# Two-layer hybrid decoder step on one core: where the second layer's modulation is loaded and computed, at what rate the convolution taps run, and which engine scales the prompt softmax

## The reference

```
mod   = silu(c) @ w_ada + b_ada ;  shift, scale, gate = split(mod, 3)     # c: 1 + 8 rows, w_ada 2048 x 6144
h     = rms_norm(x, norm_g) * (1 + scale) + shift
zq, zk, zv, zqi, zki, zwi, zga, zglu, zgc, zmerge = split(h @ w_in)
q, k  = rope(rms_norm(..)) ; qi, ki = rope(..)                            # indexer: 16 heads of 64
score = sum_heads(relu(qi . ki) * wi) ; keep the top k keys per query     # 128 (prompt), 256 (sample)
attn  = softmax(q . k over the kept keys) @ v
u     = za * sigmoid(zb) ; d = causal depthwise conv of u, 31 taps ; d = silu(layer_norm(d))
out   = (sigmoid(zma) * ((attn * silu(zga)) @ w_attn_out) + sigmoid(zmb) * ((d * silu(zgc)) @ w_conv_out)) @ w_out
x     = x + gate * out
```

## Time and profile before

| | |
|---|---|
| three runs, median (lowest, highest) | 3971.25 us (3962.26, 3978.71) |
| profiled execution, its own time | 3962.51 us |
| its span, first to last instruction | 3960.7 us |
| mean granted TensorE clock | 0.954 |
| TensorE busy | 3610.7 us (91%) |
| VectorE busy | 1882.9 us (48%) |
| GpSimd busy | 1238.9 us (31%) |
| ScalarE busy | 1033.6 us (26%) |
| DMA | 590.50 MB, mean 149 GB/s |

### The profile page before, as it was taken

One profiled execution on the slowest core, in us unless ns is written; L12 is line 12 of the kernel. 1 busy time (PEld: TensorE's weight loads), 2 busy tenths in 40 slices (PEclk: granted clock), 3 DMA queues, 4 the chain that ended last, 5 costly groups with the idle time before them and its releaser, 6 DMA issues. The chain is left out here.

```text
span 3960.7 us, 67100 instructions
## 1 busy us (share of the span) xinstructions
PE 3610.7 (91%) x27774; PEld 3312.9 (84%) x27774; DVE 1882.9 (48%) x3002; ACT 1033.6 (26%) x1430; POOL 1238.9 (31%) x476
## 2 busy tenths in 40 slices
PE   5699998888999998888987999888899899999999
PEld 2599977778889888777776999878689898899999
DVE  1413578954999123112112324679938994123301
ACT  1322222122342333111112222221223422332221
POOL 0133322444323222222222333223633232223433
PEclk8799999999999999899988999999999999999999
DMA  9633333444535674656665455443333236754442
GB/s 302 218 106 100 87 95 98 136 143 147 168 115 162 213 238 151 199 183 188 192 207 185 142 162 155 136 116 87 87 98 100 61 96 207 247 164 126 131 125 93
DMA packets 556517, 590.50 MB, mean 149 GB/s; under 512 B 73432, under 2 KB 523245, under 8 KB 546475
## 3 DMA queue, kind: packets, MB, share of 16 engines
q1 hardware_dynamic: 556212, 586.21, 49.0%
HBM read 546.37 MB, written 116.39 MB: 167 GB/s over the span
## 5 line engine op out<-in xcount | busy, mean ns | idle before, releaser
L744 POOL TENSOR_TENSOR w_lo_t<-raw,w_hi_t 128x1024 fp32r<-128x1024 f32 x472 | 1238.7, 2625 | 2705.1 <-ACT w_hi_t L753 2705.1
L1024 PE MATMUL acc<-act_hi,w_hi_t 128*128 128x272 f32 x6528 | 1438.4, 302 | 158.7 <-DVE u_s L1507 50.3
L1024 PE MATMUL acc<-act_lo,w_hi_t 128*128 128x272 f32 x6528 | 1376.2, 293 | 0.0
L1024 PE MATMUL acc<-act_hi,w_lo_t 128*128 128x272 f32 x6528 | 1375.9, 293 | 0.0
L1024 PEld LDWEIGHTS acc<-act_hi,w_hi_t 128*128 128x128 f32 x6528 | 1058.6, 194 | 260.1 <-issue 143.1
L1024 PEld LDWEIGHTS acc<-act_lo,w_hi_t 128*128 128x128 f32 x6528 | 1056.3, 194 | 0.0
L1024 PEld LDWEIGHTS acc<-act_hi,w_lo_t 128*128 128x128 f32 x6528 | 1048.2, 194 | 0.0
L753 ACT ACTIVATE w_hi_t<-raw 128x1024 fp32r<-128x1024 f32 x472 | 499.8, 1059 | 1876.8 <-PE acc L1024 1873.8
L1024 PE MATMUL acc<-m_hi,w_hi_t 128*128 128x272 f32 x1024 | 224.5, 301 | 0.0
L1024 PE MATMUL acc<-m_hi,w_lo_t 128*128 128x272 f32 x1024 | 215.8, 292 | 0.0
L1024 PE MATMUL acc<-m_lo,w_hi_t 128*128 128x272 f32 x1024 | 215.7, 292 | 0.0
(11 more groups left out here) (242 smaller groups left out, 2811.1 us busy)
## 6 DMA issues: line engine op xcount, KB each, us to landing
raw<-in_w_in_dram SPq DMA_DIRECT2D x272, 512.0 KB, 3.7
ada_ring<-in_w_ada_dram SPq DMA_DIRECT2D x155, 512.0 KB, 6.2
raw<-in_w_in_dram SPq DMA_DIRECT2D x136, 256.0 KB, 3.3
k_near<-in_cache_k_dram SPq DMA_DIRECT2D x256, 128.0 KB, 2.7
v_near<-in_cache_v_dram SPq DMA_DIRECT2D x256, 128.0 KB, 2.7
k_ring<-k_near SPq DMA_DIRECT2D x64, 512.0 KB, 5.2
v_page<-v_near SPq DMA_DIRECT2D x64, 512.0 KB, 6.0
raw<-in_w_out_dram SPq DMA_DIRECT2D x64, 512.0 KB, 3.5
```

Source lines behind the costliest of these rows:

```text
L744: pool.tensor_tensor(w_lo_t[:, m % 2], raw[:, m % 4], w_hi_t[:, m % 2].bitcast(F32), ALU.subtract).then_inc(S.w_lo, 1)
L1024: last = pe.matmul(acc[:, 2 * m + h, 0:HALF], w[:, c % 2, k, P * m:P * m + P], r[:, kt, h * HALF:(h + 1) * HALF], start=first and k == 0 a ...
```

## The change

- **Modulation.** Until group 50 one piece a chunk, then 25 pieces in 8 chunks (`ada_by`), all at the chunk's second half. Until the output groups three places, from piece 92 on eight (`ada_more`: five more in the region of `act_lo`, which is free then). Loads are issued by `ada_loads`, two chunks before the chunk of use, ahead of the other loads of `aside`; a load waits until the last piece in its place is used (`ada_before`). A block is turned in the chunk after the one that completes it (`ada_turns`). The places share eight semaphores.
- **Constants.** `H_TOK` 3 to 5, `H_SUM` 112 to 117, `H_TOPP` 125 to 130, `H_LP` 142 to 146, `H_AS` 198 to 200 (and with it `H_COMB`).
- **Taps.** One a half until 40 as before; then two a half until 64, and 16 in 5 halves from there, instead of three throughout. The last taps stand at h = 116 instead of 111. The sample columns of all eight tiles are copied once, ahead of LayerNorm, instead of once a tile.
- **Sample top-k.** The late rate is 3 in 2 halves instead of 4 in 3.
- **Token turn.** TensorE turns all keys first, then the indexer keys, then the indexer weights, instead of the three kinds for each tile of tokens.
- **Prompt scaling.** VectorE keeps the reciprocal (`rsum_done`); ScalarE multiplies, by two copies with a scale at half p_start(w) + 1.
- The wait for the staged indexer keys stands ahead of both first loads.

```diff
-H_TOK = 3
+H_TOK = 5
-H_SUM = 112
-H_TOPP = 125
-H_LP = 142
-H_AS = 198
+H_SUM = 117
+H_TOPP = 130
+H_LP = 146
+H_AS = 200
+ADA_IN_MG = 28
 def ada_slot(d):
-    return d % 7 if d < ADA_FIRST else 4 + (d - ADA_FIRST) % 3
+    if d < ADA_FIRST:
+        return d % 7
+    x = d - ADA_FIRST
+    return 4 + x % 3 if x < ADA_IN_MG else 4 + (x - ADA_IN_MG) % 8
+def ada_sem(d):
+    return ada_slot(d) % 8
+def ada_before(d):
+    return max([x + 1 for x in range(d) if ada_slot(x) == ada_slot(d)], default=0)
+def ada_by(p):
+    return ADA_FIRST + (p if p <= ADA_IN_MG else ADA_IN_MG + 25 * (p - ADA_IN_MG) // 8)
 def ada_range(n, i, half):
     p = 4 * (n - N_MG - 1) + i
-    a, b = ((ADA_FIRST + (3 * x if x <= 8 else 24 + 2 * (x - 8))) for x in (p, p + 1))
-    mid = a + (b - a + 1) // 2
-    return range(a, mid) if half == 0 else range(mid, b)
+    return range(ada_by(p), ada_by(p + 1)) if p >= 0 and half == 1 else range(0)
+def ada_turns(n, i, half):
+    p = 4 * (n - N_MG - 1) + i
+    return [d // 4 for d in range(ada_by(p - 1), ada_by(p)) if d % 4 == 3] if p >= 1 and half == 1 else []
+def ada_loads(n, i):
+    p = 4 * (n - N_MG - 1) + i
+    def begun(d):
+        use = next(x for x in range(60) if d < ada_by(x + 1))
+        return max(use - 2, 0, ADA_IN_MG if ada_slot(d) >= 7 else 0)
+    return [d for d in range(ADA_FIRST, ADA_ALL) if begun(d) == p]
 def taps_by(h):
-    return min(CT_ * TAPS, 32 + 3 * (h - 39))
+    if h < 64:
+        return 32 + 2 * (h - 39)
+    return min(CT_ * TAPS, 80 + 16 * (h - 63) // 5)
 def halves_s(h):
-    return min(64, 28 + (4 * (h - H_LP - 27) + 2) // 3)
+    return min(64, 28 + (3 * (h - H_LP - 27) + 1) // 2)
...
+        ada_more = at(8704, "ada_more", [P, 5, 4, 256])
...
             def load_ada(d):
-                if d < ADA_FIRST:
-                    need(sp, S.ada_used, d - 6)
-                else:
-                    need(sp, S.ada_used, max(ADA_FIRST, d - 2))
+                need(sp, S.ada_used, ada_before(d))
                 if d == ADA_FIRST:
                     sp.wait_ge(S.split_lo, 16)
+                if ada_slot(d) == 7:
+                    sp.wait_ge(S.w_used, w_chunk(0, N_OUT, 0))
...
+                if l == 0 and n > N_MG:
+                    for d in ada_loads(n, i):
+                        load_ada(d)
                 c = n - N_MG
...
-                if l == 0 and n > N_MG:
-                    for half in range(2):
-                        for d in ada_range(n, i, half):
-                            load_ada(d)
...
+                    if h == p_start(w) + 1:
+                        n = P * (qt + 1)
+                        act.wait_ge(S.rsum_done, 16 * l + w + 1)
+                        for x in range(2):
+                            last = act.activation(probs_p[:, w % 2, x, 0:n], probs_p[:, w % 2, x, 0:n], ACT.Copy, scale=rsum_p[:, w % 2, x:x + 1])
+                        last.then_inc(S.p_ready, 1)
...
                 for t, (t0, n) in enumerate(TT):
-                    main = t < 4
                     for h in range(KVH):
-                        out = aux[:, h, t0:t0 + n] if main else aux[0:n, 3, P * h:P * h + P]
+                        out = aux[:, h, t0:t0 + n] if t < 4 else aux[0:n, 3, P * h:P * h + P]
                         pe.transpose(out, k_new[:, h, t0:t0 + n], ident)
-                    out = aux[:, 2, ID * t:ID * t + ID] if main else aux[0:n, 3, 256:256 + ID]
+                for t, (t0, n) in enumerate(TT):
+                    out = aux[:, 2, ID * t:ID * t + ID] if t < 4 else aux[0:n, 3, 256:256 + ID]
                     pe.transpose(out, ki_new[0:ID, t0:t0 + n], ident[0:ID, 0:ID])
-                    if main:
-                        pe.transpose(aux[:, 2, 256 + IH * t:256 + IH * t + IH], wi_new[:, t0:t0 + n], ident[0:IH, 0:IH])
+                for t, (t0, n) in enumerate(TT[:4]):
+                    pe.transpose(aux[:, 2, 256 + IH * t:256 + IH * t + IH], wi_new[:, t0:t0 + n], ident[0:IH, 0:IH])
...
-                        if d % 4 == 1 and d > ADA_FIRST + 1:
-                            turn_rows(d // 4 - 1)
+                    for e in ada_turns(n, i, half):
+                        turn_rows(e)
...
-                    st.then(dve.tensor_copy(conv[:, c, SEQ:TOK], d_s[:, c, :]))
...
-                st.then(dve.reciprocal(rsum_p[:, s, :], sum_p[:, s, :]))
-                st.wait()
-                for x in range(2):
-                    last = dve.tensor_scalar(probs_p[:, s, x, 0:n], probs_p[:, s, x, 0:n], rsum_p[:, s, x:x + 1], None, ALU.mult)
-                last.then_inc(S.p_ready, 1)
+                dve.reciprocal(rsum_p[:, s, :], sum_p[:, s, :]).then_inc(S.rsum_done, 1)
...
                 if s == 0:
+                    st.wait()
+                    st.then(dve.tensor_copy(conv[:, 0:CT_, SEQ:TOK], d_s[:, :, :]))
```

More of the change, by code:

```diff
@@ L164 @@
 ADA_ALL = 192
+ADA_IN_MG = 28
 def ada_slot(d):
-    return d % 7 if d < ADA_FIRST else 4 + (d - ADA_FIRST) % 3
-def ada_landed_at(d):
-    return 16 * sum(1 for x in range(d + 1) if ada_slot(x) == ada_slot(d))
+    if d < ADA_FIRST:
[4 more added lines that the diff above has]
+    return ada_slot(d) % 8
+def ada_landed_at(d):
+    return 16 * sum(1 for x in range(d + 1) if ada_sem(x) == ada_sem(d))
+def ada_before(d):
+    return max([x + 1 for x in range(d) if ada_slot(x) == ada_slot(d)], default=0)
+def ada_by(p):
+    return ADA_FIRST + (p if p <= ADA_IN_MG else ADA_IN_MG + 25 * (p - ADA_IN_MG) // 8)
 def ada_range(n, i, half):
     p = 4 * (n - N_MG - 1) + i
-    if p < 0:
-        return range(0)
-    a, b = ((ADA_FIRST + (3 * x if x <= 8 else 24 + 2 * (x - 8))) for x in (p, p + 1))
-    mid = a + (b - a + 1) // 2
-    return range(a, mid) if half == 0 else range(mid, b)
+    return range(ada_by(p), ada_by(p + 1)) if p >= 0 and half == 1 else range(0)
[8 more added lines that the diff above has]
+    return [d for d in range(ADA_FIRST, ADA_ALL) if begun(d) == p]
 def taps_by(h):
@@ L402, in ada_place @@
         def ada_place(d):
-            return raw[:, ada_slot(d)] if ada_slot(d) < 4 else ada_ring[:, ada_slot(d) - 4]
+            s = ada_slot(d)
+            return raw[:, s] if s < 4 else ada_ring[:, s - 4] if s < 7 else ada_more[:, s - 7]
         names = """w_landed0 w_landed1 w_landed2 w_landed3 w_hi w_lo w_used m0_done acc0_free acc1_free
@@ L407, in trunk_kernel @@
             sq_ready ssq_added ssq_ps rstd_x hs_ready hs_hi h_lo h_mid h_hi x_first x_kept0 x_kept1
-            ada_landed0 ada_landed1 ada_landed2 ada_landed3 ada_landed4 ada_landed5 ada_landed6 ada_used ada_rowed mod_turned mod_done
+            ada_landed0 ada_landed1 ada_landed2 ada_landed3 ada_landed4 ada_landed5 ada_landed6
+            ada_landed7 ada_used ada_rowed mod_turned mod_done
             aux_ready swap_used std_ready rope_done tok_turned tok_done tok_stored
@@ L413, in trunk_kernel @@
             gate_stored0 gate_stored1 gate_stored2 gate_stored3 ga_used
-            bias_done bias_stored logits_p praw_done exp_p p_ready ptr_p ptc_p pv_p ao_p
+            bias_done bias_stored logits_p praw_done exp_p rsum_done p_ready ptr_p ptc_p pv_p ao_p
             k_landed0 k_landed1 k_landed2 k_turned k_cp_a k_cp_b qblk_done logits_s brep_in0 brep_in1 sraw_done exp_s ps_ready pts_ps pts_done
@@ L422, in trunk_kernel @@
         acc_free = [S.acc0_free, S.acc1_free]
-        ada_landed = [S.ada_landed0, S.ada_landed1, S.ada_landed2, S.ada_landed3, S.ada_landed4, S.ada_landed5, S.ada_landed6]
+        ada_landed = [S.ada_landed0, S.ada_landed1, S.ada_landed2, S.ada_landed3, S.ada_landed4, S.ada_landed5, S.ada_landed6, S.ada_landed7]
         kx_landed, state_in, u_stored = [S.kx_landed0, S.kx_landed1], [S.state_in0, S.state_in1], [S.u_stored0, S.u_stored1]
@@ L492, in load_ada @@
                 sp.dma_start(ada_place(d), w_ada[l, 512 * i:512 * i + 512, 256 * g:256 * g + 256].rearrange(
-                    "(t p) n -> p t n", p=P)).then_inc(ada_landed[ada_slot(d)], 16)
+                    "(t p) n -> p t n", p=P)).then_inc(ada_landed[ada_sem(d)], 16)
             def load_state(l, c):
@@ L505, in load_kx @@
                     sp.wait_ge(S.dots_ready, 32 * l + 32)
+                    sp.wait_ge(S.kx_staged, 16 * DEPTH * SEQS * PAGES)
                 else:
                     sp.wait_ge(S.kx_turned, 8 * l + b - 1)
-                    if b == 0:
-                        sp.wait_ge(S.kx_staged, 16 * DEPTH * SEQS * PAGES)
                 for f in range(2):
@@ L1037, in ada @@
                 e, i = divmod(d, 4)
-                pe.wait_ge(ada_landed[ada_slot(d)], ada_landed_at(d))
+                pe.wait_ge(ada_landed[ada_sem(d)], ada_landed_at(d))
                 if i == 0:
@@ L1613, in norm_p @@
             def norm_p(l, w):
-                n, s = P * (P_UNITS[w][0] + 1), w % 2
+                s = w % 2
                 dve.wait_ge(S.exp_p, 16 * l + w + 1)
-                st.then(dve.reciprocal(rsum_p[:, s, :], sum_p[:, s, :]))
-                st.wait()
-                for x in range(2):
```

(8 more changed lines are left out.)

## The result

The changed kernel takes 3795.65 us (median of four runs, 3791.70 to 3803.81); the kernel before, run beside it, takes 3967.55 (3962.26 to 3978.71). The ratio is 0.9575, 95% interval 0.9552 to 0.9597. The forecast was 3800, range 3735 to 3860. The profiled execution took 3799.16 us, 163.4 less than that of before (3962.51).

What follows compares the result with a forecast made beforehand. TensorE's own work plus its pauses was taken as the bound (busy 3610.7 of 3960.7 us). 3962.5 - 131.4 (modulation) - 39 (two layers) = 3792, plus 8.7 for the median: 3801, said as 3800, range 3735 to 3860.

Steps and rivals of the forecast that it cites:

- Modulation, -131.4: Layer 0's merge and output: pieces asked for two chunks early; 15 groups go from 606.2 to 474.8 us, 131.4 saved.
- Rival C: Modulation stays late or slow in the output stage, by SP hanging or a clock drop: 75 us, 3875; chance 0.10.
- Token turn, -8 a layer: At half 5 the 4.21 us wait for rotated queries goes, about 2 of slow matmuls too; sorting saves 2.3.
- Taps and u_s, -17 a layer: After half 40, two taps a half instead of three cut TensorE's u_s waits by 15, and about 2 of clock.
- GpSimd's waits, 0: TensorE's 47.2 us of waits for POOL's w_lo_t stay: 0, with -30 and +40 a kernel as ends.
- Rival E: Taps and POOL fall out of step, and the w_lo_t waits go with their clock (47.2 + 15): 3738; chance 0.11.
- rival B: Longer tap streams hold POOL out more often, 60: 3860; or VectorE's late start eats the u_s gain: 3830; chance 0.14.
- Softmax later, +4.4: Variance to first softmax: TensorE arrives one half earlier, waits 3.0 longer; two gate multiplications add 0.7 each; +4.4 a layer.
- top-k, +6.0: Sample top-k before the key copy: the same 38 steps get 29 halves instead of 31; +6.0 a layer.
- scaling -3: Prompt attention: 64 multiplications move from VectorE to ACT; -3 a layer, bounds -6 a layer and +7 a unit.
- shift -2: Last attention matmuls shift past the last window half: -2 a layer, bounds -2 and +2.
- Rival D: ACT waits for the reciprocal and scales before making w_hi; TensorE waits 7 us a unit, 224: 4024; chance 0.03.

Runs made afterwards that it cites:

- the holes: On the changed kernel, every fourth convolution tap waits for the tap right before it instead of the one before that; 3740.50 us, ratio 0.9450 to the kernel before.

## Why the prediction was right, point by point

- **Modulation, -131.4: right, -133.4.** Groups of 27.5 were forecast and measured. Output groups of 32.5 to 33 were forecast, 32.0 to 34.0 measured. The price of pieces without a wait (0.75 for the first, 0.47 for each further) held, and so did the full clock. When the waits went, the clock rose to 1.00, in the seven output groups even with 87 pieces where 56 stood, so the 32-column pieces themselves do not lower it. The Trainium skill (TensorE: Matmul & The Clock Gate, "HAM oscillation") says that DMA waits between short bursts of matmuls make the clock fall again and again. The trace agrees in the waits, though the stretches between them were not short: before, they stood some 20 us apart in the merge, with a clock of 0.90. The last group took 52.7, not 50.9. Rival C is refuted: a wait of 0.9 and one of 0.64 where it needed 16; taking five places away brings it back in part (15 waits, 20.5 us).
- **Token turn, -8 a layer: right, -9.9 and -10.0.** The wait went and no new one came; the sorting saved 1.6 us of the turn (5.78 to 4.14, both behind the wait) where I took 2.3.
- **Taps and u_s, -17 a layer: right, -17.7 and -22.2**, and undone alone it costs 12.9 and 13.8 before half 64.
- **GpSimd's waits, 0: right in sum, by luck of the draw between parts.** Halves 72 to 103 lost 3.5 and 6.3 us; a 12.6 us wait at half 106 of layer 0 is absent after, but also when only the modulation is changed. The total went from 47.2 to 42.4. (By the rate the first stream holds 124 taps, not the 121 of the forecast.) That GpSimd waits for some 20 taps and not for one is shown: the holes remove it. Rival E's 3738 is what its absence is worth, and the kernel with the holes, 3740.5, is at that price; rival B did not occur here, but its mechanism is real (63.3 us with a stream of 4.5 taps a half).
- **Softmax later, +4.4; top-k, +6.0; scaling -3; shift -2: +5.4 a layer after half 120, and +18.1 and +10.5 were measured.** This is the step that failed, by 18 us over two layers. Its terms: the k_t wait grew from 4.2 to 9.1, +4.9 against a forecast of 6.0, right; but a wait for the key pages of 2.8 came behind it in layer 0, SyncE's order again, and the group's clock is 0.89. The npeak_p wait grew from 7.5 to 9.9, less than the forecast near 12. The forecast let TensorE arrive at the softmax one half earlier with nothing in its way, and that is what failed. The lines of the variance, of one gate and of the first softmax:

```profile
977.51 1.08 PE L1076 MATMUL aux<-ln_sum,con 128*128 128x272 f32 x4
...
1013.59 0.73 DVE L1833 TENSOR_TENSOR conv<-conv,gate 128x544 f32<-128x544 f32 x1 [2.96 <-ACT gate L853]
...
1061.51 0.29 DVE L1650 CUSTOM_DVE_ANT_0 probs_p<-aux,bias_p 128x128 f32<-128x128 f32 x1 [0.15 <-DVE bias_p L1625]
```

  VectorE's stretch takes 84.0 us where it took 77.4. I had counted 1.4 for the two gate multiplications that fall into it. VectorE waited 2.96 for the gate of one, and the four are busy 4.4 us where the two of before were 1.4, which makes 6.0 of the 6.6. (The 77.4 were not without a pause, as I had read: VectorE waited 4.7 in them for ln_rstd.) TensorE needed 74.9 us from the variance to the point where it waits, where it had needed 70.7: 4.2 later instead of 3.0 earlier, so only 2.4 of VectorE's 6.6 show as a longer npeak_p wait. It was held 4.3 us on the way by ACT's gate at half 128, and ran the group behind it at a clock of 0.89 (0.94 in layer 1) instead of 1.00. Halves 120 to 127 alone take 5.9 and 6.1 more. These 12 us over the two layers, which the forecast put at nothing, are most of the 18. ScalarE's timeline shows what the gate stands behind:

```profile
978.84 1.28 ACT L920 ACT_TABLE_LOAD   x1
980.13 0.72 ACT L920 ACTIVATE ln_rstd<-aux,eps 128x544 f32<-128x544 f32 x1
980.87 1.28 ACT L924 ACT_TABLE_LOAD   x1
985.23 1.57 ACT L924 ACTIVATE conv<-conv,par 128x544 f32<-128x544 f32 x2 [3.08 <-DVE conv L1776]
986.82 1.28 ACT L853 ACT_TABLE_LOAD   x1
988.11 0.62 ACT L853 ACTIVATE gate<-acc 128x544 f32<-128x544 f32 x1
```

  With the variance at half 125, LayerNorm's square root and the silu of its first two tiles, with a wait of 3.08 for VectorE and three table loads of 1.28, come just ahead of that gate; with the variance at half 120 they stood behind the group's gates. The wait for ln_sum, 5.7 a layer at half 119, was put at nothing too; before it was 2.3 in layer 1 alone. Halves 104 to 119 of layer 1 take only 0.5 more for it, since that 2.3 and a gate's wait of 1.8 are gone from there. The scaling gave nothing that shows instead of 3. With the LayerNorm at its old place and its taps in time all of these waits go, 25 a layer.
- **The sum.** -133.4 for -131.4, and -30.0 for -39 outside: ahead of half 72 the gain was 7 larger than forecast, behind half 120 it was 18 smaller. And halves 104 to 111 of layer 0 gave 15.0 of the 30.0, by the w_lo_t wait of 12.6 that was in the trace of before; it is also absent with the modulation part alone, so no run shows that the change removed it. Without it the profiled gain outside is 15 for a forecast of 39, and that these executions came out near the sum is in part luck. For the profiled execution the sum said 3792 and it took 3799.2. The median lay 3.5 below it this time, where I had put it 8.7 above as before, and that too is why the forecast of 3800 stands closer to 3795.65 than its terms deserve.

Rival D did not occur: moving the scaling back to VectorE changes the median by 1.8 us.

## What to carry to other kernels

Price a transfer's lateness by the pace of the rows without a wait, bare group plus so much a piece, and give it places for the chunk in which most pieces are used. When a wait on one engine is taken away, look what stands in the queue of the next one, SyncE's as well: twice here a second wait stood right behind the first. Where a long stream of VectorE instructions overlap each other, let one in four wait for its predecessor: it cost VectorE 0.12 us for each such wait (start to start 0.78 for 0.66) and gave the kernel 50 to 55.

## What the runs showed of the hardware

- GpSimd's subtraction is held out as long as VectorE's two-input instructions overlap (start to start 0.66, duration 0.74 us), up to 18.13 us for one that takes 2.39 alone. A start 0.78 behind the last one, a hole of 0.04 us, lets it in. With such holes the longest is 3.21.
- With 115 pieces of 128*32 matmuls beside the weights the granted clock is 1.00 for the 420 us of merge and output; with three places 16.6 us of waits in the output, the longest 3.8, go with 0.96.
- The ten 128x128 turns take 1.25 us at a granted clock of 1.00, and 2.40 at 0.50 behind a wait of 4.21.
